# In whole tiles of the products by features, the high-part matmuls of both halves first, then the low-part ones of both

## The chip, the cores and the metric

The kernel runs on one NeuronCore of a Trainium2 chip. Its engines are TensorE (PE, with its weight loads PEld), VectorE (DVE), ScalarE (ACT), GpSimd (POOL) and SyncE (SP), which issues the transfers. Matmul results go to PSUM, which has eight banks of 128 partitions by 512 float32 columns. The metric is the device time in microseconds of one execution.

## The reference

A sequence of 256 positions with 1024 features, all float32, passes through two blocks. Of the first, two layers: attention over chunks of 64 frames, then a gated linear recurrence with a short convolution, each followed by an MLP with squared ReLU. The second block puts three mixers beside each other (gated linear attention, sparse attention that picks its keys by an index score, cross attention to 256 memory positions) and adds them by gates.

```
h  = h + attention(rmsnorm(h)) ; h = h + (relu(rmsnorm(h) @ w1) ** 2) @ w2
h  = h + rglru(rmsnorm(h))     ; h = h + (relu(rmsnorm(h) @ w1) ** 2) @ w2
u  = rmsnorm(x) @ w_in         # q, k, v, gates ... of three mixers, 11352 columns
x  = x + rmsnorm((s1 * y1 @ w1o + s2 * y2 @ w2o + s3 * y3 @ w3o) @ w_o)
```

Nearly all the work is products of a 256 x 1024 activation with weights. The result needs more precision than one fast matmul gives.

## The kernel before, in words

**Splitting.** Every operand is cut in a high part (rounded to the fast 32-bit format, `fp32r`) and a low part (the rest), and a product is the sum high x high + high x low + low x high. Weights come in tiles of 128 x 2048 (1 MB). SP loads a tile into one of five `raw` buffers. ACT makes `hi` of it (L822, two halves of a tile, three buffers `hi`), DVE makes `lo` (L1349, in place of `raw`). The semaphores `hi_cut` and `lo_cut` count these halves.

**Products by features.** Their output has features on the partitions and the 256 positions in the columns: q, k, w1 of the MLPs, rin, and most of the second block's first product. A tile holds the weights of 2 x 128 output features (j = 0, 1: the two halves in this case's words) for all 1024 input features, as NC = 8 blocks k of 128. The activation `X2` keeps for each block its high part and its low part side by side, 512 columns. So one matmul of 512 columns (`high`, L338) gives high x high in columns 0 to 255 of a bank and high x low in columns 256 to 511; one of 256 columns with the low weights (`low`, L346) adds low x high to columns 0 to 255. Each half of a tile takes 8 high and 8 low matmuls and has a bank of its own. `half` (L329) does one half: 7 highs, 8 lows, the last high. `cols` (L353) does a whole tile as two calls of `half`, one after the other.

**Draining.** When the last matmul of a bank tells `filled`, ACT copies columns 256 to 511 into a buffer `bt` (L853, three buffers), and DVE adds `bt` to columns 0 to 255 (`joined`, L1363 or, with a scale, L1365). DVE's sum tells `freed` of the bank. In `dv` it is ACT's copy alone that frees the bank (L833).

**Banks.** `fill(key, b)` makes PE wait until the bank's last contents have been drained (`freed[b]`), and books the next one. A `Side` object leaves out a wait that the same engine has passed before.

**Order.** Each engine has one queue, written out by hand in the program and worked in order. The ways in which `cols` follows other work on PE are:
- MLP: `cols` of w1 tile i, on banks (4,5) (tile 1 on (6,7)), then `rows` of w2 tile i-1 on banks 0 to 3 (24 matmuls of 512 columns, L293 to L295), then w1 tile i+1.
- rin 1 to 3: banks (2,3), (4,5), (2,3), with the small `gates` matmuls between.
- start of the second block: iq 0 on (4,5) (`cols_as_ready`), misc on bank 0, iq 1 on (4,5); index heads, dk and dq 0 half by half; dv on banks 4 and 5 (48 matmuls of 256 columns); then `cols` of dq 1, dq 2, gq 0, gq 1, gk 0, all on (4,5), and gk 1 on (0,1).
- dz 0 to 3: banks (4,5), (0,1), (4,5), (0,1), after the `gv` tiles.
- wk 0 on (4,5) and wq 0 on (7,6) near the start; xz 0 on (2,3), followed by xz 1's first half on bank 2.

In the stretch of dq, gq and gk DVE also takes maxima of the index scores (`top8`) after the two sums of each tile.

Of the kernel before, what the change touches and what calls it, by code (L numbers as in the profile page):

```python
# [8 lines left out]
P = 128  # L9
S = 256  # L10
D = 1024
NC = D // P
# [6 lines left out]
RAW, HIS, BT = 5, 3, 3  # L19
# [42 lines left out]
T_OF = {key: t for t, key in enumerate(PLAN)}  # L62
# [28 lines left out]
def build(nc, A, out):  # L91
    ctx = ExitStack()

    def sem(name):
        return ctx.enter_context(nc.semaphore(name))

    raw_in = [sem(f"raw_in{i}") for i in range(RAW)]
    hi_cut, lo_cut, tile_used = sem("hi_cut"), sem("lo_cut"), sem("tile_used")
# [44 lines left out]
    def place(name, off, free, dt=F32):  # L143
        return nc.alloc_sbuf_tensor_at(name, [P] + list(free), dt, offset=off)
# [5 lines left out]
    lo = [place(f"lo_{i}", o_raw + i * 8192, [TILE], F32R) for i in range(RAW)]  # L150
    hi = [place(f"hi_{i}", o_hi + i * 8192, [TILE], F32R) for i in range(HIS)]

    def slot(name, i, free=(NC, S), dt=F32, off=0):
        return place(name, o_slot[i] + off, free, dt)
# [63 lines left out]
    ik, low = slot("ik", 5, [S]), slot("low", 5, [S], off=1024)  # L218
# [30 lines left out]
    bank = [ctx.enter_context(nc.psum_tensor(f"bank{i}", [P, 512], F32)) for i in range(8)]  # L249
# [9 lines left out]
    full, free, bank_of, tile_end, bt_at = {}, {}, {}, {}, {}  # L259

    def cut_at(t, c):

        return 2 * (t - 2) + c + 1
# [7 lines left out]
    def pe():  # L271
        PE = nc.tensor
        p = Side(PE)
# [3 lines left out]
        def fill(key, b, read=None):  # L277
            if b in read_by:
                p.wait_ge(*read_by.pop(b))
            p.wait_ge(freed[b], reads[b])  # L280
            fills[b] += 1
            full[key], bank_of[key] = (filled[b], fills[b]), bank[b]
            if key[0] in ROWS_ADDED:
                read_by[b] = (h_added, ROWS_ADDED[key[0]] + b + 1)
            elif read:
                read_by[b] = read
            else:
                reads[b] += 1
                free[key] = (freed[b], reads[b])
            return filled[b]  # L290

        def mm3(o, ah, al, bh, bl, start, stop):
            PE.matmul(o, ah, bh, start=start, stop=False)  # L293
            PE.matmul(o, ah, bl, start=False, stop=False)  # L294
            return PE.matmul(o, al, bh, start=False, stop=stop)  # L295
# [33 lines left out]
        def half(name, i, j, x, b, ks=range(NC), last=False):  # L329
            t = T_OF[name, i]  # L330
            if ks[0] == 0:
                fill((name, 2 * i + j), b)
            wh, wl = hi[t % HIS], lo[t % RAW]

            def high(k_):
                p.wait_ge(hi_cut, cut_at(t, k_ // 4))
                c = k_ * 256 + j * 128
                return PE.matmul(bank[b][:, :], wh[:, c:c + P], x[:, k_, :, :].rearrange("p a b -> p (a b)"),  # L338
                                 start=k_ == 0, stop=k_ == NC - 1, skip_group_check=True)

            for k_ in ks[:-1]:
                high(k_)
            for k_ in ks:
                p.wait_ge(lo_cut, cut_at(t, k_ // 4))
                c = k_ * 256 + j * 128
                PE.matmul(bank[b][:, 0:S], wl[:, c:c + P], x[:, k_, 0, :], start=False, stop=False, skip_group_check=True)  # L346
            m = high(ks[-1])
            if ks[-1] == NC - 1:
                m.then_inc(filled[b], 1)
                if j == 1 or last:  # L350
                    tile_end[t] = full[name, 2 * i + j]

        def cols(name, i, x, banks):  # L353
            half(name, i, 0, x, banks[0])
            half(name, i, 1, x, banks[1])

        def cols_as_ready(name, i, x, banks, split):
            t = T_OF[name, i]
# [144 lines left out]
        total("mix0", 0)  # L503
        p.wait_ge(ident_in, 16)
        cols("wk", 0, X2, (4, 5))
        cols("wq", 0, X2, (7, 6))
        for b in range(4):
            p.wait_ge(*free["wv", b])
# [29 lines left out]
        for j in range(9):  # L538
            name, i = ATTN_TILES[j]
# [22 lines left out]
        def mlp(n, fill_i):  # L562
            p.wait_ge(x_low, low_at("mem", NC - 1))
            half("mk", fill_i, 0, M2, 7)
            turned_x(f"mlp{n}", h, h_added, 8 * n)
            half("mk", fill_i, 1, M2, 6)
            for i in range(17):
                if i == 0:
                    cols_as_ready(f"w1_{n}", 0, X2, (4, 5), f"mlp{n}")
                elif i < 16:  # L570
                    cols(f"w1_{n}", i, X2, (6, 7) if i == 1 else (4, 5))
                if i > 0:
                    p.wait_ge(z_low, 32 * n + 2 * i)
                    rows(f"w2_{n}", i - 1, 16, zh[(i - 1) % 3], zl[(i - 1) % 3])
# [40 lines left out]
        done = fill(("iw", 0), 1)  # L615
        for j in range(2):
            m = PE.transpose(bank[1][:, 32 * j:32 * j + 32], low[0:32, j * P:(j + 1) * P], ident[0:32, 0:32])
# [18 lines left out]
        t = T_OF["dv", 0]  # L636
        for j in range(2):
            done = fill(("dv", j), 4 + j)
            for k_ in range(NC):
                p.wait_ge(lo_cut, cut_at(t, k_ // 4))  # L640
                w, r = slice(k_ * 256, (k_ + 1) * 256), slice(j * P, (j + 1) * P)
                m = mm3(bank[4 + j][:, 0:S], xh[:, k_, r], xl[:, k_, r], hi[t % HIS][:, w], lo[t % RAW][:, w],
                        k_ == 0, k_ == NC - 1)
# [25 lines left out]
        for i in range(10):  # L669
# [11 lines left out]
            if i >= 2:  # L681
                n = i - 2
                c = (n // 4) * 128
                p.wait_ge(*free["turn", 16 + n])
                done = fill(("dav", n), 7)
# [48 lines left out]
        for i in range(6):  # L734
# [5 lines left out]
            if i < 4:  # L740
                p.wait_ge(mk_low, i + 1)
                p.wait_ge(xq_low, i + 1)
                done = fill(("s", 24 + i), 4)
                for j, c in ((1, 0), (0, 256)):
                    for k_ in range(2):
# [3 lines left out]
                        m = PE.matmul(o, xql[:, n, r], mkh[:, n, :], start=False, stop=k_ == 1, skip_group_check=True)  # L749
# [3 lines left out]
            if i >= 2:  # L753
# [3 lines left out]
                for m_ in range(2):  # L757
                    b = 6 + m_
                    done = fill(("xo", 2 * n + m_), b)
                    c = n * 256 + m_ * P  # L760
                    for j in range(2):
                        r = slice(j * 256, j * 256 + 256)
                        m = mm3(bank[b][:, 0:S], mvh[:, j, c:c + P], mvl[:, j, c:c + P], pth[n % 2][:, r], ptl[n % 2][:, r], j == 0, j == 1)
# [26 lines left out]
        for s_, c in ((0, 0), (0, 1), (1, 0), (1, 1)):  # L790
            r = slice(s_ * P, (s_ + 1) * P)
            for i in (2, 3):
                t = T_OF["wf", i]
                p.wait_ge(f_low, i + 1)
                for k_ in range(2):
                    p.wait_ge(lo_cut, cut_at(t, k_))
                    w = slice(k_ * D + c * 512, k_ * D + (c + 1) * 512)
                    m = mm3(bank[2 * c + s_][:, :], fh[:, 2 * i + k_, r], fl[:, 2 * i + k_, r], hi[t % HIS][:, w], lo[t % RAW][:, w],
                            False, i == 3 and k_ == 1)
# [1370 lines left out]
```

## Time and profile before

| | us |
|---|---|
| three runs | 977.11, 977.18, 975.89 (median 977.11) |
| profiled execution, its span | 975.9 |
| PE busy | 968.3 (99%) |
| PEld busy | 826.0 (85%) |
| DVE busy | 680.5 (70%) |
| ACT busy | 588.6 (60%) |
| matmuls L338, x1016, mean 394 ns | 266.3 |
| matmuls L346, x1016, mean 282 ns | 141.6 |

The times of the runs lie within 1.3 us. The profiled execution's time is its span, 975.9, and no more stands beside it: the lowest of the three runs, 975.89, agrees with it. The duration of a matmul is modelled and overlaps the next one, so the distance of two starts is what a matmul costs, not its 394 or 282 ns. The profile groups matmuls of one line that follow each other: "209.35 2.00 PE L338 ... x8" is the last high of one half and the first seven of the next.

### The profile page before, as it was taken

The page shows a single profiled execution, that of the slowest core. Times are in us where ns is not written, and L with a number is a line of the kernel's source. Part 1 is how long each engine was busy: PE and PEld are TensorE (multiplying, and loading weights), DVE is VectorE, ACT ScalarE, POOL GpSimd, SP SyncE. Part 2 cuts the span into 40 slices and gives each one's busy share as a digit, 9 for nine tenths or more (in the row PEclk, how much of TensorE's full clock was granted, in tenths as well). Part 3 has the DMA queues.
Part 4 walks back from the last instruction along what each step waited for, and adds up shares of the span by engine and source line. Part 5 has one row for each costly group of instructions (what it writes and reads, how often), then busy time and mean ns, then how long its engine had stood idle before and what let it go on. Part 6 is the DMA issues. An engine that isn't in the chain of part 4 may idle for free.

```text
span 975.9 us, 13399 instructions
## 1 busy us (share of the span) xinstructions
PE 968.3 (99%) x5146; PEld 826.0 (85%) x5146; DVE 680.5 (70%) x1161; ACT 588.6 (60%) x1042; POOL 66.2 (7%) x80
## 2 busy tenths in 40 slices
PE   8999999999999999999999999999999999999997
PEld 6887788888888898888888888888888888988886
DVE  5877786666568789666665588778767554877564
ACT  6777755454457897645454467547876555684443
POOL 1322110000000242000000000000011000000000
PEclk9999999999999999999999999999999999999999
DMA  9753545655455445555655556445543544335551
GB/s 368 296 194 134 184 173 186 224 176 211 174 196 185 146 165 192 182 187 184 226 178 207 177 198 250 173 175 188 198 165 105 193 148 170 132 133 209 177 189 44
DMA packets 27119, 180.33 MB, mean 185 GB/s; under 512 B 2992, under 2 KB 3888, under 8 KB 6320
## 3 DMA queue, kind: packets, MB, share of 16 engines
q1 hardware_dynamic: 26336, 176.98, 50.7%
q0 software_dynamic: 288, 2.10, 0.6%
q8 instruction: 41, 0.67, 0.3%
q10 hardware_dynamic: 432, 0.39, 0.1%
q14 instruction: 22, 0.18, 0.0%
HBM read 178.41 MB, written 1.05 MB: 184 GB/s over the span
## 4 chain that ended last, share of the span: by engine, by line
PE 99%; DMA 1%; DVE 0%; ACT 0%; SPq 0%; issue 0%; DVEq 0%
PE bank L338 25%; PE bank L293 16%; PE bank L295 16%; PE bank L294 16%; PE bank L346 13%; PE bank L308 1%; PE bank L468 1%; PE bank L484 1%; PE bank L589 1%; PE bank L518 1%; PE bank L309 1%; DMA front<-in_front 1%; PE bank L529 1%; PE bank L404 0%; PE bank L399 0%; PE bank L400 0%
## 5 line engine op out<-in xcount | busy, mean ns | idle before, releaser
L1349 DVE TENSOR_TENSOR lo<-raw,hi 128x1024 fp32r<-128x1024 f32 x318 | 375.9, 1229 | 20.1 <-ACT hi L822 19.9
L822 ACT ACTIVATE hi<-raw 128x1024 fp32r<-128x1024 f32 x318 | 320.3, 1050 | 100.1 <-PE bank L295 98.2
L338 PE MATMUL bank<-X,hi 128*128 128x512 f32 x1016 | 266.3, 394 | 0.0
L338 PEld LDWEIGHTS bank<-X,hi 128*128 128x128 f32 x1016 | 185.0, 189 | 32.8
L346 PEld LDWEIGHTS bank<-X,lo 128*128 128x128 f32 x1016 | 138.5, 190 | 10.1
L346 PE MATMUL bank<-X,lo 128*128 128x256 f32 x1016 | 141.6, 282 | 0.0
L853 ACT ACTIVATE bt<-bank 128x256 f32<-128x256 f32 x135 | 51.0, 380 | 141.5 <-PE bank L338 133.1
L1363 DVE TENSOR_TENSOR zr<-bank,bt 128x256 f32<-128x256 f32 x64 | 27.2, 424 | 108.9 <-ACT bt L853 108.9
L293 PE MATMUL bank<-hi,zh 128*128 128x512 f32 x256 | 100.0, 390 | 0.0
L295 PE MATMUL bank<-hi,zl 128*128 128x512 f32 x256 | 99.8, 390 | 0.0
L294 PE MATMUL bank<-lo,zh 128*128 128x512 f32 x256 | 99.6, 389 | 0.0
L293 PE MATMUL bank<-hi,X 128*128 128x512 f32 (+1 forms) x176 | 67.9, 386 | 0.0
L295 PE MATMUL bank<-hi,X 128*128 128x512 f32 (+1 forms) x176 | 66.9, 380 | 0.0
L294 PE MATMUL bank<-lo,X 128*128 128x512 f32 (+1 forms) x176 | 66.8, 380 | 0.0
L295 PEld LDWEIGHTS bank<-hi,zl 128*128 128x128 f32 x256 | 48.1, 188 | 10.4
L294 PEld LDWEIGHTS bank<-lo,zh 128*128 128x128 f32 x256 | 48.1, 188 | 10.2
L293 PEld LDWEIGHTS bank<-hi,zh 128*128 128x128 f32 x256 | 48.2, 188 | 8.8
L997 ACT ACTIVATE zh<-zf 128x256 fp32r<-128x256 f32 x64 | 26.6, 416 | 21.3 <-DVE zf L1520 21.3
L295 PEld LDWEIGHTS bank<-hi,X 128*128 128x128 f32 x176 | 33.1, 188 | 6.4
L293 PEld LDWEIGHTS bank<-hi,X 128*128 128x128 f32 x176 | 33.1, 188 | 6.2 <-issue 0.3
L294 PEld LDWEIGHTS bank<-lo,X 128*128 128x128 f32 x176 | 33.1, 188 | 6.0
L907 ACT ACTIVATE L<-L,stat 128x256 f32<-128x256 f32 (+1 forms) x56 | 25.5, 457 | 20.4 <-DVE stat L1482 9.8
(345 smaller groups left out, 1420.5 us busy)
## 6 DMA issues: line engine op xcount, KB each, us to landing
raw<-in_w SPq DMA_DIRECT2D x64, 1024.0 KB, 4.7
raw<-in_rin SPq DMA_DIRECT2D x8, 1024.0 KB, 4.8
raw<-in_wk SPq DMA_DIRECT2D x4, 1024.0 KB, 10.3
raw<-in_wq SPq DMA_DIRECT2D x4, 1024.0 KB, 8.3
raw<-in_wo SPq DMA_DIRECT2D x4, 1024.0 KB, 4.7
raw<-in_mk SPq DMA_DIRECT2D x4, 1024.0 KB, 4.8
raw<-in_mv SPq DMA_DIRECT2D x4, 1024.0 KB, 4.8
raw<-in_rout SPq DMA_DIRECT2D x4, 1024.0 KB, 4.6
```

The source lines that it names most:

```text
L293: PE.matmul(o, ah, bh, start=start, stop=False)
L294: PE.matmul(o, ah, bl, start=False, stop=False)
L295: return PE.matmul(o, al, bh, start=False, stop=stop)
L308: PE.matmul(bank[b][:, :], wh[:, c:c + P], both_, start=k_ == 0, stop=False, skip_group_check=True)
L338: return PE.matmul(bank[b][:, :], wh[:, c:c + P], x[:, k_, :, :].rearrange("p a b -> p (a b)"), start=k_ == 0, stop=k_ == NC - 1, skip_gro ...
L346: PE.matmul(bank[b][:, 0:S], wl[:, c:c + P], x[:, k_, 0, :], start=False, stop=False, skip_group_check=True)
L822: ACTE.activation(hi[u_ % HIS][:, c], raw[u_ % RAW][:, c], ACT.Copy).then_inc(hi_cut, 1)
L853: ACTE.activation(bt[n % BT][:, :], bank_of[key][:, S:2 * S], func, scale=scale, **kw).then_inc(bt_made, 1)
L907: i = ACTE.activation(Lb[:, c:e], Lb[:, c:e], ACT.Exp, scale=-1.0, bias=s_[:, m:m + 1], accum_out=s_[:, 2 + m:3 + m])
L997: ACTE.activation(zh[i % 3][:, j, :], zf[c % 4][:, :], ACT.Copy).then_inc(z_high, 1)
L1349: DVE.tensor_tensor(lo[u_ % RAW][:, c], raw[u_ % RAW][:, c], hi[u_ % HIS][:, c].bitcast(F32), ALU.subtract).then_inc(lo_cut, 1)
L1363: DVE.tensor_tensor(dst, first, rest, ALU.add).then_inc(free[key][0], 1)
```

## The change

`cols` no longer calls `half` twice. It fills both banks first, then issues 8 highs into the first bank, 7 into the second, 8 lows into the first (the last of them tells `filled` of the first bank), 8 lows into the second, and the second bank's last high, which tells `filled` of the second. The matmuls, their operands and their count are the same; within a bank the sums are added in another order. `half` stays as it is for the tiles that are done half by half. The lines of the kernel after the change stand 26 lower from here on, and the whole tiles' highs and lows are now on L362 and L368.

```diff
@@ -351,8 +351,34 @@
                     tile_end[t] = full[name, 2 * i + j]
 
         def cols(name, i, x, banks):
-            half(name, i, 0, x, banks[0])
-            half(name, i, 1, x, banks[1])
+
+            t = T_OF[name, i]
+            wh, wl = hi[t % HIS], lo[t % RAW]
+            done = [fill((name, 2 * i + j), banks[j]) for j in range(2)]
+
+            def high(j, k_):
+                p.wait_ge(hi_cut, cut_at(t, k_ // 4))
+                c = k_ * 256 + j * 128
+                return PE.matmul(bank[banks[j]][:, :], wh[:, c:c + P], x[:, k_, :, :].rearrange("p a b -> p (a b)"),
+                                 start=k_ == 0, stop=j == 1 and k_ == NC - 1, skip_group_check=True)
+
+            def low(j, k_):
+                p.wait_ge(lo_cut, cut_at(t, k_ // 4))
+                c = k_ * 256 + j * 128
+                return PE.matmul(bank[banks[j]][:, 0:S], wl[:, c:c + P], x[:, k_, 0, :], start=False,
+                                 stop=j == 0 and k_ == NC - 1, skip_group_check=True)
+
+            for k_ in range(NC):
+                high(0, k_)
+            for k_ in range(NC - 1):
+                high(1, k_)
+            for k_ in range(NC):
+                m = low(0, k_)
+            m.then_inc(done[0], 1)
+            for k_ in range(NC):
+                low(1, k_)
+            high(1, NC - 1).then_inc(done[1], 1)
+            tile_end[t] = full[name, 2 * i + 1]
 
         def cols_as_ready(name, i, x, banks, split):
             t = T_OF[name, i]
```

PE's order at the passage from dq 1 to dq 2, where both tiles use banks 4 and 5. Names: `hi_2_61` is the tile's high part in the third `hi` buffer, `lo_2_56` its low part, `X2_91` the activation; a bracket holds the semaphores that the row waits for. Before:

```order
L338 MATMUL bank5<-X2_91,hi_1_60 128x512
L338 MATMUL bank4<-X2_91,hi_2_61 128x512 [waits hi_cut,freed4]
L338 MATMUL bank4<-X2_91,hi_2_61 128x512 x3
L338 MATMUL bank4<-X2_91,hi_2_61 128x512 [waits hi_cut]
L338 MATMUL bank4<-X2_91,hi_2_61 128x512 x2
L346 MATMUL bank4<-X2_91,lo_2_56 128x256 [waits lo_cut]
L346 MATMUL bank4<-X2_91,lo_2_56 128x256 x3
L346 MATMUL bank4<-X2_91,lo_2_56 128x256 [waits lo_cut]
L346 MATMUL bank4<-X2_91,lo_2_56 128x256 x3
L338 MATMUL bank4<-X2_91,hi_2_61 128x512
L338 MATMUL bank5<-X2_91,hi_2_61 128x512 [waits freed5]
```

After the change, the same passage:

```order
L368 MATMUL bank5<-X2_91,lo_1_55 128x256 x8
L362 MATMUL bank5<-X2_91,hi_1_60 128x512
L362 MATMUL bank4<-X2_91,hi_2_61 128x512 [waits hi_cut,freed5,freed4]
L362 MATMUL bank4<-X2_91,hi_2_61 128x512 x3
L362 MATMUL bank4<-X2_91,hi_2_61 128x512 [waits hi_cut]
L362 MATMUL bank4<-X2_91,hi_2_61 128x512 x3
L362 MATMUL bank5<-X2_91,hi_2_61 128x512 x7
```

What moved: the wait for `freed5` stood before the second half's first high, 7 highs and 8 lows and one high into dq 2, and now stands with `freed4` at dq 2's first matmul. The second bank's highs follow the first's without lows between.

PE's order in the first MLP, from the middle of a w1 tile (banks 4, 5) to the w2 rows behind it (bank 0, with `zh`, `zl`: the two parts of the squared ReLU). Before:

```order
L346 MATMUL bank4<-X2_91,lo_0_54 128x256 [waits lo_cut]
L346 MATMUL bank4<-X2_91,lo_0_54 128x256 x3
L338 MATMUL bank4<-X2_91,hi_0_59 128x512
L338 MATMUL bank5<-X2_91,hi_0_59 128x512 [waits freed5]
L338 MATMUL bank5<-X2_91,hi_0_59 128x512 x6
L346 MATMUL bank5<-X2_91,lo_0_54 128x256 x8
L338 MATMUL bank5<-X2_91,hi_0_59 128x512
L293 MATMUL bank0<-hi_1_60,zh0_124 128x512 [waits lo_cut,z_low]
```

After the change:

```order
L362 MATMUL bank5<-X2_91,hi_0_59 128x512 x7
L368 MATMUL bank4<-X2_91,lo_0_54 128x256 [waits lo_cut]
L368 MATMUL bank4<-X2_91,lo_0_54 128x256 x3
L368 MATMUL bank4<-X2_91,lo_0_54 128x256 [waits lo_cut]
L368 MATMUL bank4<-X2_91,lo_0_54 128x256 x3
L368 MATMUL bank5<-X2_91,lo_0_54 128x256 x8
L362 MATMUL bank5<-X2_91,hi_0_59 128x512
L293 MATMUL bank0<-hi_1_60,zh0_124 128x512 [waits lo_cut,z_low]
```

What moved: two runs of highs and two of lows are now one of each, with one high at the end; the rows of w2 behind the tile, and what they wait for, stand as before.

## Rows read from the trace of the kernel before

**Rows 1.** The page, busy time by engine, and its chain by engine
```profile
PE 968.3 (99%) x5146; PEld 826.0 (85%) x5146; DVE 680.5 (70%) x1161; ACT 588.6 (60%) x1042; POOL 66.2 (7%) x80
...
PE 99%; DMA 1%; DVE 0%; ACT 0%; SPq 0%; issue 0%; DVEq 0%
```

**Rows 2.** Waits of PE and its weight loads: us in total, times, longest
```profile
PE bank L496 <- POOL warm L1995: 1.3, 1, 1.3
PE bank L378 <- ACT hi L920: 1.1, 1, 1.1
...
PEld bank L293 <- DVE lo L1349: 0.3, 1, 0.3
```

**Rows 3.** Order of time on PE, an MLP tile: start, us, engine, line, idle before
```profile
206.81 1.75 PE L338 MATMUL bank<-X,hi 128*128 128x512 f32 x7
208.39 1.12 PE L346 MATMUL bank<-X,lo 128*128 128x256 f32 x8
209.35 2.00 PE L338 MATMUL bank<-X,hi 128*128 128x512 f32 x8
211.19 1.11 PE L346 MATMUL bank<-X,lo 128*128 128x256 f32 x8
...
212.37 0.40 PE L293 MATMUL bank<-hi,zh 128*128 128x512 f32 x1
```

**Rows 4.** Busy time by stretches: PE, PEld, DVE, ACT, POOL, granted clock, DMA
```profile
0.00:10.00 10.00, 7.53 (x19) 4.23 (x20) 3.10 (x7) 4.65 (x8) 0.74 (x5) 1.00 0.80 291
...
629.00:658.00 29.00, 29.00 (x169) 25.55 (x168) 19.46 (x43) 13.65 (x21) 0.00 (x0) 1.00 0.51 181
```

**Rows 5.** Order of time on PE, from dv to gk 0
```profile
623.76 0.28 PE L293 MATMUL bank<-hi,X 128*128 128x256 f32 x1
...
629.52 1.78 PE L338 MATMUL bank<-X,hi 128*128 128x512 f32 x7
...
634.88 2.00 PE L338 MATMUL bank<-X,hi 128*128 128x512 f32 x8
...
640.47 2.00 PE L338 MATMUL bank<-X,hi 128*128 128x512 f32 x8
...
657.23 2.00 PE L338 MATMUL bank<-X,hi 128*128 128x512 f32 x8
```

**Rows 6.** Order of time on DVE, bank 5 drained after that MLP tile
```profile
201.96 0.42 DVE L1363 TENSOR_TENSOR zr<-bank,bt 128x256 f32<-128x256 f32 x1 [1.91 <-ACT bt L853]
```

**Rows 7.** DVE's sums of iq 0, and PE at the start of iq 1
```profile
602.23 0.76 DVE L1363 TENSOR_TENSOR iq<-bank,bt 128x256 f32<-128x256 f32 x2
...
603.09 2.00 PE L338 MATMUL bank<-X,hi 128*128 128x512 f32 x8
```

**Rows 8.** Order of time on ACT at dq 1 and dq 2
```profile
629.72 0.38 ACT L833 ACTIVATE dv<-bank 128x256 f32<-128x256 f32 x1 [2.49 <-PE bank L295]
...
635.32 0.38 ACT L853 ACTIVATE bt<-bank 128x256 f32<-128x256 f32 x1 [2.41 <-PE bank L338]
```

**Rows 9.** Order of time on DVE at dq 1 and dq 2
```profile
635.73 0.43 DVE L1365 SCALAR_TENSOR_TENSOR dq<-bank,bt 128x256 f32<-128x256 f32 x1 [2.37 <-ACT bt L853]
...
641.32 0.42 DVE L1365 SCALAR_TENSOR_TENSOR dq<-bank,bt 128x256 f32<-128x256 f32 x1 [1.39 <-ACT bt L853]
```

**Rows 10.** ACT's release and PE's restart near 9 us
```profile
8.57 0.61 ACT L920 ACTIVATE hi<-front 128x512 fp32r<-128x512 f32 x1
...
9.24 0.73 PE L378 MATMUL bank<-hi,X 128*128 128x512 f32 x2 [1.14 <-ACT hi L920]
9.81 0.40 PE L381 MATMUL bank<-hi,X 128*128 128x512 f32 x1
```

**Rows 11.** PE at xz 0 and xz 1, and DVE's second sum
```profile
822.66 1.75 PE L338 MATMUL bank<-X,hi 128*128 128x512 f32 x7
...
827.99 1.32 PE L338 MATMUL bank<-X,hi 128*128 128x512 f32 x5
...
828.84 0.42 DVE L1363 TENSOR_TENSOR zx<-bank,bt 128x256 f32<-128x256 f32 x1 [2.08 <-ACT bt L853]
```

## The prediction

> **What bounds the kernel now.** I read the page first: matmuls fill 968.3 of 975.9 us and the chain that ended last is 99% PE [rows 1]. Busy PE alone proves little, since matmuls are pipelined, so next I read what PE waited for: two waits in the whole execution, the longest 1.3 us, for the first constants and for the first `hi` [rows 2]. Then the order of time inside a tile: matmuls of 512 columns start 0.227 us apart (7 from 206.81 to 208.39) and those of 256 columns 0.12 us apart (8 from 208.39 to 209.35), with nothing between them [rows 3]. The granted clock is 1.00, the 2.4 GHz level [rows 4]. So PE's instruction stream is the bound. Work of ACT and DVE counts only where it makes PE wait, and a PE wait anywhere is added to the end, because no later slack can swallow it.
>
> **What is only moved.** Each of the 47 whole tiles keeps its 32 matmuls: 16 high ones of 512 columns, 16 low ones of 256. (wk 1, wq 1, w1 of both MLPs 30, rin 3, iq 1, dq 2, gq 2, gk 2, dz 4, xz 1.) No other engine gets or loses an instruction, and no DMA is touched. Three things change: how often PE passes from a low run into a high run, when the first bank is complete, and when the second bank has to be free.
>
> **Term 1, runs.** After a low run the highs come a little slower: 8 from 209.35 to 211.19 take 1.84 us, against 8 x 0.2266 = 1.81 at the pace of the 7 before [rows 3]. Seen by halves: first high 206.81, first high of the second half 209.35 + 0.23 = 209.58, next group of rows 212.37, so 2.77 us for the half that starts clean and 2.79 for the one that starts behind lows. The change takes one such passage out of each tile, the one in its middle; that at its end stays. 47 x 0.02 = 0.94, or 1.03 with the unrounded starts behind these rows. I take -1.0 us. Bounds: nothing (0) and, if both the passages of a tile went, -2.1. The longer low run of 16 should cost nothing of its own: 48 matmuls of 256 columns from 623.76 to 629.52 are 0.120 apart too [rows 5].
>
> **Term 2, low parts later.** The lows start after 15 highs in place of 7, 1.8 us later, so VectorE's `lo` gets more time. The only wait for `lo` is one of 0.3 us before a weight load of L293, the products by rows [rows 2], none in these tiles, so this gives 0.
>
> **Term 3, the second bank.** `half` asked for its bank when it began; `cols` now asks for both before its first matmul. The order of PE shows this: `freed5` moves from the middle of the tile to its first row. It is asked for 2.77 us sooner. Where another group of matmuls lies between two uses of the bank this is free. In the MLPs, DVE frees bank 5 at 201.96 + 0.42 = 202.38, and the next `w1` tile starts at 206.81 [rows 3, 6]: 4.4 us to spare, 30 tiles alike but for the alternation at i = 1. `dz` alternates (4,5) and (0,1), so that a whole tile of 5.6 us lies between two uses of a bank. iq 1: 602.23 + 0.76 = 602.99 against 603.09 + 0.23 = 603.32 [rows 7].
> It is not free where tiles on banks (4,5) stand back to back: dv, dq 1, dq 2, gq 0, gq 1, gk 0. That is five entries.
> - dv to dq 1: dq 1 starts at 629.52 [rows 5]; bank 5 holds dv's second half, which ACT copies from 629.72 for 0.38, free at 630.10 [rows 8]. PE would idle 0.58 us.
> - dq 1 to dq 2: the last high of dq 1 starts at 634.88, the first of dq 2 at 635.11 [rows 5]. The bank is freed by two engines in turn: ACT's `bt` at 635.32 for 0.38 [rows 8], DVE's sum at 635.73 for 0.43, free at 636.16 [rows 9]. PE would idle 1.05 us. Gq 0 repeats it: last high 640.47 [rows 5], DVE done 641.32 + 0.42 [rows 9]; gq 1 and gk 0 have the same distance. Four entries. DVE is free when `bt` comes: the first half's sum will start some 4.9 us into the tile and end 0.7 us before the second's is due.
>
> Restart: the second wait of [rows 2], in mid-work, shows it. ACT's `hi` ends at 8.57 + 0.61 = 9.18, matmul restarts at 9.24 and the next two starts lie 0.57 us on, not 0.45, since the first weight load was not under a matmul [rows 10]. So about 0.05 + 0.11 = 0.16 us each. The highs after an idle PE do not pay the 0.03 of term 1. Sum: (0.58 + 0.16 - 0.03) + 4 x (1.05 + 0.16 - 0.03) = 0.71 + 4.72 = +5.4 us. Bounds: without any restart +4.6; with twice that restart +6.2.
>
> The TensorE page of the Trainium skill ("TensorE: Matmul & The Clock Gate", Part 2, LDWEIGHTS step) says that PE's queue can pull weight loads ahead of matmuls in flight. If it did so past a wait for a bank, 0.11 of each restart would go and the sum would be 0.55 us less. [Rows 10] speak against it: there the next two starts come 0.57 us on, the time of one load over the usual.
>
> **Term 4, the first bank.** It is complete after 15 highs and 8 lows, 15 x 0.2266 + 8 x 0.12 = 4.35 us into the tile; before it was 2.77. Its drain ends about 1.2 us after its last matmul starts, so 5.4 us in, and the tile lasts 5.56. Only xz 0 is followed at once by a user of its first bank: start 822.66, last low 826.90, `bt` 827.22, DVE from 827.63 (idle there, 2.08 us before 828.84) to 828.05; xz 1 starts at 828.20 [rows 11]. That is just in time; if the weight load has to wait too it costs 0.05. I take 0, bound +0.3. Elsewhere ACT and DVE drain the pair closer together, but the last drain of a tile hangs on the second half, whose end stays: `z` in the MLP waits for it, k and q in the attention, the taps of rin.
>
> **Sum.** -1.0 + 0 + 5.4 + 0 = +4.4 us against the profiled execution's 975.9, its span, which agrees with the lowest of the three times (975.89); so 980.3. The median of the runs is 977.1, 1.2 above, so a median of 981.5. Bounds: -2.1 + 4.6 = +2.5 and 0 + 6.2 + 0.3 = +6.5.
>
> **Rivals.**
> - A, not slower: the early wait has no price. The place is the start of dq 1, dq 2, gq 0, gq 1 and gk 0; it decides if bank 5 is free within 0.23 us of the last high's start. Then term 1 alone is left, 977.1 - 1.0 = 976.1. For it: PE shows no bank wait now. Against it: ACT's `bt` starts 0.43 us after that high's start (634.88 to 635.32) and two operations of 0.4 us follow each other [rows 5, 8, 9]; it can't be free before 1.2. Chance 0.05. To gain more, all passages between runs would have to cost over 0.11 us a tile (5.4 / 47), and the rows have 0.05 at most; 0.02 for that, at 974.9.
> - B, clock: a PE that idles 1.2 us in each 6.7 loses granted clock in this stretch. Price: work of 28 us (five tiles, 629.52 to 657.23 + 0.23 [rows 5]) at the 1.2 GHz level takes twice as long, +28 us if all of it, +7 for a quarter; with term 3, 988 to 1010. Against it: PE idled 1.14 us before 9.24 and the granted clock is 1.00 in 0 to 10 us as well [rows 4, 10]. Chance 0.04. The same page of the Trainium skill, in its section on a second HAM failure mode, says that small idles between groups of matmuls can make the clock swing; by that rule this rival would hold.
> - C, more entries bite than the five: iq 1 (0.33 us to spare), xz 1 (0.15), or VectorE behind at one of them, since its queue is in order and it now drains both halves together. Up to 1.2 us each, +1 to +3 over the forecast, 982.5 to 984.5. Against it: DVE's rows show idle time before both sums there [rows 9]. Chance 0.12.
> - D, that the change does not do what it says: the order of PE shows it does; 0.
>
> **Numbers.** The forecast, 979.5 to 983.5 around 981.5, has 0.77; A 0.05 and 0.02, B 0.04, C 0.12. The range for 8 in 10 takes the bounds of the terms (+2.5 to +6.5: 979.6 to 983.6), half of C, and the 0.6 us by which medians may lie apart: 979.2 to 984.3. A change of 0.2%, 1.95 us, is what a measurement of this kernel can tell from none. Slower by more: the forecast but for its lowest edge, B and C, 0.91; within: A and that edge, 0.07; faster 0.02.
>
> **What would show it.** In the profile after: idle time of PE or its weight loads before the high matmuls of five tiles between 629 and 665 us, released by DVE `dq`, `gq` (ACT `dv` the first time), 0.6 once and about 1.1 four times; tile starts there 6.7 us apart, not 5.59. In the MLP a `w1` tile of 5.54 plus 0.02 us, and stage starts some 0.8 us earlier by 600 us. Wrong would be: no such waits (A), a granted clock under 1 (B), waits in `w1`, iq or xz tiles (C), or a low run of 16 slower than 1.92 us, which would undo term 1.

## The result, and the profile after

The changed kernel takes 982.11 us (median of five runs, 981.48 to 982.30), the kernel before 977.18 us in the same session. The ratio is 1.0049, interval [1.0037, 1.0061]: 0.5% slower. The profiled execution of the changed kernel spans 980.8 us at a granted clock of 1.00, that of before 975.9.

The page after: the busy time by engine, one group of matmuls, and the shares of the chain that ended last.

```profile
PE 969.7 (99%) x5146; PEld 826.8 (84%) x5146; DVE 680.9 (69%) x1161; ACT 589.4 (60%) x1042; POOL 66.3 (7%) x80
...
PE 98%; DMA 1%; issue 0%; DVE 0%; ACT 0%; SPq 0%; DVEq 0%
...
L362 PE MATMUL bank<-X,hi 128*128 128x512 f32 x752 | 186.6, 391 | 4.4 <-issue 4.4
```

The work is the same (5146 matmuls, as in [rows 1]). New is the idle time of 4.4 us before the highs of the whole tiles. The waits after, first PE's, then the first row of its weight loads (us in total, times, longest):

```profile
PE bank L362 <- issue: 4.4, 5, 1.0
PE bank L522 <- POOL warm L2021: 1.3, 1, 1.3
PE bank L404 <- ACT hi L946: 0.3, 1, 0.3
...
PEld bank L362 <- issue: 5.8, 5, 1.3
```

Against [rows 2] one wait is new, and it comes five times. The profile names no releaser ("issue" is time for which it shows no reason), so the list alone doesn't say what PE waited for. PE in order of time, from dq 1 to gk 0, does better:

```profile
628.90 0.28 PE L295 MATMUL bank<-hi,X 128*128 128x256 f32 x1
629.71 3.68 PE L362 MATMUL bank<-X,hi 128*128 128x512 f32 x15 [0.52 <-issue]
633.22 2.08 PE L368 MATMUL bank<-X,lo 128*128 128x256 f32 x16
635.14 0.39 PE L362 MATMUL bank<-X,hi 128*128 128x512 f32 x1
636.51 3.65 PE L362 MATMUL bank<-X,hi 128*128 128x512 f32 x15 [0.98 <-issue]
...
641.91 0.39 PE L362 MATMUL bank<-X,hi 128*128 128x512 f32 x1
643.28 3.67 PE L362 MATMUL bank<-X,hi 128*128 128x512 f32 x15 [0.98 <-issue]
646.78 2.08 PE L368 MATMUL bank<-X,lo 128*128 128x256 f32 x16
...
656.83 3.65 PE L362 MATMUL bank<-X,hi 128*128 128x512 f32 x15 [0.98 <-issue]
...
662.23 3.14 PE L362 MATMUL bank<-X,hi 128*128 128x512 f32 x13
```

The five idles stand at the first highs of dq 1, dq 2, gq 0, gq 1 and gk 0, one of 0.52 and four of 0.98. (The view counts an idle from the modelled end of the matmul before, 0.39 us after its start; the next high could have started 0.23 after it, so an idle of 0.98 keeps PE 1.14 longer.) Tile starts lie 6.8 us apart where they lay 5.59 apart [rows 5]. Who ends such an idle is seen at gq 0, by the same view of the weight loads, ACT and DVE:

```profile
643.25 0.76 PEld L362 LDWEIGHTS bank<-X,hi 128*128 128x128 f32 x4 [1.26 <-issue]
```
```profile
641.15 0.38 ACT L879 ACTIVATE bt<-bank 128x256 f32<-128x256 f32 x1 [3.31 <-PE bank L368]
642.34 0.38 ACT L879 ACTIVATE bt<-bank 128x256 f32<-128x256 f32 x1 [0.81 <-PE bank L362]
```
```profile
641.57 0.42 DVE L1391 SCALAR_TENSOR_TENSOR dq<-bank,bt 128x256 f32<-128x256 f32 x1 [1.72 <-ACT bt L879]
642.75 0.42 DVE L1391 SCALAR_TENSOR_TENSOR dq<-bank,bt 128x256 f32<-128x256 f32 x1 [0.76 <-ACT bt L879]
```

The last high of dq 2 starts at 641.91. ACT copies from 642.34, DVE adds from 642.75 and is done with bank 5 at 643.17. The weight load starts at 643.25 and the matmul at 643.28: unrounded, 0.07 and 0.10 behind the sum's end. These answer to [rows 8, 9], with the same distances (high to `bt` 0.43, `bt` to sum 0.41): the drain hasn't changed, only the moment at which PE asks for the bank.

The MLP tile, PE in order of time, against [rows 3]:

```profile
206.82 3.56 PE L362 MATMUL bank<-X,hi 128*128 128x512 f32 x15
210.22 2.08 PE L368 MATMUL bank<-X,lo 128*128 128x256 f32 x16
212.13 0.40 PE L362 MATMUL bank<-X,hi 128*128 128x512 f32 x1
212.36 0.40 PE L293 MATMUL bank<-hi,zh 128*128 128x512 f32 x1
```

The tile takes 212.36 - 206.82 = 5.54 us, before 212.37 - 206.81 = 5.56. From one w1 tile's start to the next (tile and w2 rows, 26 such steps in the two MLPs, each within 0.001 of the mean) it is 11.007 us after and 11.027 before: 0.020 won. Its start stands where it stood, because this execution was 0.2 us behind in the first ten us (9.42 for the matmul that started at 9.24 in [rows 10]) and has won that back over the tiles since.

**Where the 4.9 us went.** Matched matmul by matmul, the changed kernel is 0.19 us late at 10 us, 0.50 early at dv, 5.00 late at gk 1, 4.9 at xz 0 and 4.95 at the end. So the five entries cost 5.5 us net, the 36 whole tiles ahead of them win 0.71, 0.0196 each, and what is left is the start: from the 10th us to the end the change costs 4.77. Busy time by engine in this stretch shows nothing but idle PE (30.57 us busy of 35); the granted clock, the third number from the end, is 1.00:

```profile
629.00:664.00 35.00, 30.57 (x169) 25.94 (x168) 20.23 (x47) 14.64 (x22) 0.00 (x0) 1.00 0.45 152
```

### The profile page after: what moved, and what is told of

It is laid out like the page before. It is cut to its first block, busy times and chain, and to the rows that moved or that the text cites. A ratio compares the mean times of both kernels' runs of the same rounds, so it can differ in the third digit from the quotient of the medians.

```text
span 980.8 us, 13401 instructions
## 1 busy us (share of the span) xinstructions
PE 969.7 (99%) x5146; PEld 826.8 (84%) x5146; DVE 680.9 (69%) x1161; ACT 589.4 (60%) x1042; POOL 66.3 (7%) x80
## 3 DMA queue, kind: packets, MB, share of 16 engines
HBM read 178.41 MB, written 1.05 MB: 183 GB/s over the span
## 4 chain that ended last, share of the span: by engine, by line
PE 98%; DMA 1%; issue 0%; DVE 0%; ACT 0%; SPq 0%; DVEq 0%
PE bank L362 18%; PE bank L293 16%; PE bank L295 16%; PE bank L294 16%; PE bank L368 9%; PE bank L338 8%; PE bank L346 4%; PE bank L308 1%; PE bank L494 1%; PE bank L510 1%; PE bank L615 1%; PE bank L544 1%; DMA front<-in_front 1%; PE bank L309 1%; PE bank L555 1%
## 5 line engine op out<-in xcount | busy, mean ns | idle before, releaser
L362 PE MATMUL bank<-X,hi 128*128 128x512 f32 x752 | 186.6, 391 | 4.4 <-issue 4.4
L362 PEld LDWEIGHTS bank<-X,hi 128*128 128x128 f32 x752 | 140.7, 188 | 32.9 <-issue 5.8
L368 PEld LDWEIGHTS bank<-X,lo 128*128 128x128 f32 x752 | 96.4, 191 | 3.7
L368 PE MATMUL bank<-X,lo 128*128 128x256 f32 x752 | 97.5, 283 | 0.0
L338 PE MATMUL bank<-X,hi 128*128 128x512 f32 x264 | 72.5, 401 | 0.0
L338 PEld LDWEIGHTS bank<-X,hi 128*128 128x128 f32 x264 | 47.5, 189 | 8.2
```

The lines of the kernel that those rows point to most:

```text
L362: return PE.matmul(bank[banks[j]][:, :], wh[:, c:c + P], x[:, k_, :, :].rearrange("p a b -> p (a b)"), start=k_ == 0, stop=j == 1 and k_ = ...
L368: return PE.matmul(bank[banks[j]][:, 0:S], wl[:, c:c + P], x[:, k_, 0, :], start=False, stop=j == 0 and k_ == NC - 1, skip_group_check=True)
```

## The experiments

All nine edits concern `cols` or the banks it is given; none leaves work out. The first four ran on one chip beside the kernel before (977.24), the next four on one beside it again (977.37), the ninth beside 977.23. In the changed kernels' lists of waits below, those for the first constants and the first `hi` are left out.

**e1: the new order, the second bank asked for when its first high comes.**

```diff
-            done = [fill((name, 2 * i + j), banks[j]) for j in range(2)]
+            done = [fill((name, 2 * i), banks[0])]
...
             for k_ in range(NC):
                 high(0, k_)
+            done.append(fill((name, 2 * i + 1), banks[1]))
```

> The new order of highs and lows, but PE asks for the second bank only before that bank's first high, 8 highs (1.8 us) into the tile. Bank theory (the loss is the early question for the second bank): the five waits between 629 and 660 us are gone, since a bank is free about 1.28 us after its last high starts and is now asked for 2.0 us after it; what is left is the gain of one passage from lows to highs in each of 47 tiles, 47 x 0.02 = 0.94 us, less 0.05 at xz 1: 0.9 us under the kernel before, 976.3. Order theory (the loss comes from the long runs and from ACT and DVE draining both halves together): PE still idles in this stretch and the time stays near 982.

Measured: 975.87 us, ratio 0.9988 [0.9979, 0.9997], span 975.0, no wait for a bank in the list. PE at the same place:

```profile
628.58 0.28 PE L295 MATMUL bank<-hi,X 128*128 128x256 f32 x1
628.70 3.59 PE L362 MATMUL bank<-X,hi 128*128 128x512 f32 x15
632.13 2.08 PE L368 MATMUL bank<-X,lo 128*128 128x256 f32 x16
634.04 3.85 PE L362 MATMUL bank<-X,hi 128*128 128x512 f32 x16
637.73 2.08 PE L368 MATMUL bank<-X,lo 128*128 128x256 f32 x16
```

Asking eight matmuls later takes the whole loss away and leaves a gain: 1.4 us in the medians, with 0.9 us of uncertainty, and 0.67 us between the 10th us and the end of the profiled executions, matmul by matmul. The order of the matmuls isn't what costs.

**e2: the old order, both banks asked for at the start.**

```diff
-            half(name, i, 0, x, banks[0])
-            half(name, i, 1, x, banks[1])
+            for j in range(2):
+                fill((name, 2 * i + j), banks[j])
+            half(name, i, 0, x, banks[0], filled_before=True)
+            half(name, i, 1, x, banks[1], filled_before=True)
```

> The order of the kernel before (7 highs, 8 lows, a high, twice), but both banks are asked for ahead of the tile's first matmul. Bank theory: the same five waits as in the changed kernel, 0.6 and four of 1.1 us with restart, +5.5 us in all and none of the gain of the runs: 982.7, some 0.9 above the changed kernel. The first bank is drained early here, so xz 1 doesn't wait. Order theory: no loss to speak of, 977 to 978.

Measured: 982.82 us, ratio 1.0058 [1.0045, 1.0071], span 981.5. Its waits:

```profile
PE bank L338 <- issue: 4.4, 5, 1.0
...
PEld bank L338 <- issue: 5.8, 5, 1.3
```

The same five waits, the same 4.4 and 5.8 us, without any reordering: the early asking alone makes them. The two experiments and the two kernels make a square: asked for late, old and new order take 977.2 and 975.9; asked for early, 982.8 and 982.1. The early asking costs 5.6 in the old order and 6.2 in the new; the new order gains 1.4 and 0.7, which at this uncertainty are one number. Matched matmul by matmul from the 10th us on, the square closes better: the early asking costs 5.54 in the old order and 4.77 + 0.67 = 5.44 in the new, the new order gains 0.67 and 5.54 - 4.77 = 0.77.

**e3: the changed kernel, with dq 1, gq 0 and gk 0 on banks 2 and 3.**

```diff
-            cols("dq", i, X2, (4, 5))
+            cols("dq", i, X2, (2, 3) if i == 1 else (4, 5))
...
-            cols("gq", i, X2, (4, 5))
+            cols("gq", i, X2, (4, 5) if i else (2, 3))
...
-        cols("gk", 0, X2, (4, 5))
+        cols("gk", 0, X2, (2, 3))
```

> The changed kernel with both banks asked for at the tile's start, but dq 1, gq 0 and gk 0 on banks (2,3), dq 2 and gq 1 on (4,5), so that no bank is used twice in a row. Bank theory: PE asks for banks that were last used a tile (5.5 us) ago and finds them free; no waits, 0.9 us under the kernel before, 976.3, the same as with the late question. If the question itself cost time at each of the 47 tiles, or if draining both halves together did, this one would stay above the kernel before.

Measured: 976.01 us, ratio 0.9989 [0.9980, 0.9998]. PE in this stretch:

```profile
632.90 3.82 PE L362 MATMUL bank<-X,hi 128*128 128x512 f32 x16
636.56 2.08 PE L368 MATMUL bank<-X,lo 128*128 128x256 f32 x16
638.47 3.82 PE L362 MATMUL bank<-X,hi 128*128 128x512 f32 x16
```

Still asked for early, but the bank was last used a tile ago: no wait, tile starts 5.57 apart. It is the bank's return that decides, not the wait as an instruction. (The span of this execution, 973.7, flatters it by 1.3 us that it won in the first ten us; its median doesn't show them. From there on it gains 0.85.)

**e4: asked for after 4 highs.**

```diff
             for k_ in range(NC):
+                if k_ == 4:
+                    done.append(fill((name, 2 * i + 1), banks[1]))
                 high(0, k_)
```

> The new order, with the second bank asked for after 4 highs (0.91 us into the tile). Bank theory: a bank is free 1.28 us after its last high starts; PE comes to the question 0.23 + 0.91 = 1.14 us after it, so four waits shrink to 0.14 plus the restart (0.10 until the matmul starts and 0.08 for the weight load), about 0.3 each, 1.2 in all, and the one behind dv (free 0.58 us into the tile) is gone: 977.2 - 0.9 + 1.2 = 977.5. If instead a wait has a fixed price whatever its length, the loss would stay near 5 us or vanish whole.

Measured: 977.68 us, ratio 1.0005 [0.9996, 1.0014]. The list of PE's waits shows nothing here; that of its weight loads does, and the order of time says how long:

```profile
PEld bank L362 <- DVE dq L1393: 0.9, 2, 0.4
PEld bank L362 <- DVE gq L1391: 0.9, 2, 0.4
```
```profile
634.30 4.14 PE L362 MATMUL bank<-X,hi 128*128 128x512 f32 x16
638.27 2.08 PE L368 MATMUL bank<-X,lo 128*128 128x256 f32 x16
```

Sixteen highs take 3.97 us where e1's take 3.69: 0.28 for each of four entries, 1.1 in all, and the matched matmuls are 1.13 later over the stretch. (dq 1, where the bank is back sooner, has none.) Three points give the curve of one entry, each set against e1's tile starts of 5.60: asked for after no highs 1.19 us (tile starts 6.78 apart in the changed kernel), after four 0.28, after eight nothing. Between the first two it falls by 0.91, for 4 x 0.227 = 0.91 us of later asking: one for one.

**e5: the old halves in shorter runs, 4 highs, 4 lows, 3 highs, 4 lows, 1 high.** This asks what the 0.02 of term 1 hangs on.

```diff
-            for k_ in ks[:-1]:
-                high(k_)
-            for k_ in ks:
...
+            n = len(ks) // parts
+            for at in range(0, len(ks), n):
+                for k_ in ks[at:at + n]:
+                    if k_ != ks[-1]:
+                        high(k_)
+                for k_ in ks[at:at + n]:
...
-            half(name, i, 0, x, banks[0])
-            half(name, i, 1, x, banks[1])
+            half(name, i, 0, x, banks[0], parts=2)
+            half(name, i, 1, x, banks[1], parts=2)
```

> The kernel before, but each half of a whole tile as 4 highs, 4 lows, 3 highs, 4 lows, a high: four passages from lows to highs in a tile in place of two, banks asked for as before. If each passage costs 0.02 us, whatever the length of the low run, the time rises by 2 x 0.02 x 47 = 1.9 us to 979.1. If the price grows with the low run before it, half the run has half the price and the time stays at 977.2. If the order of highs and lows has no price at all, 977.2 too, and the highs behind lows show no slower starts.

Measured: 977.19 us beside 977.37, ratio 1.0000 [0.9992, 1.0009]. The MLP tile:

```profile
206.65 1.07 PE L338 MATMUL bank<-X,hi 128*128 128x512 f32 x4
207.56 0.64 PE L349 MATMUL bank<-X,lo 128*128 128x256 f32 x4
208.03 0.86 PE L338 MATMUL bank<-X,hi 128*128 128x512 f32 x3
208.73 0.64 PE L349 MATMUL bank<-X,lo 128*128 128x256 f32 x4
209.20 1.32 PE L338 MATMUL bank<-X,hi 128*128 128x512 f32 x5
...
212.24 0.40 PE L293 MATMUL bank<-hi,zh 128*128 128x512 f32 x1
```

The step from one w1 tile to the next is 11.033 us, 0.007 over before, with four low runs in a tile in place of two. Two passages more for 0.007: a fixed 0.020 for each is out. Taken at 0.020 behind eight lows (term 1), the mean of these four is (0.040 + 0.007) / 4 = 0.012. But the edit shortens two things, the runs of lows and the runs of highs behind them, and this mean doesn't tell which counts. The distances of single starts say more (unrounded, mean of 27 w1 tiles). In the kernel before, the highs behind eight lows start 233, 236, 228, 233 and 231 ns apart before they are back at 227: 28 ns lost. The lows behind highs start 113 and 119 ns apart before they are at 120: 8 won, which leaves the 0.020. In e5 the three highs behind the first four lows start 233, 236 and 228 ns apart, as slow as behind eight, and then the next lows end the run. At the tile's end, where w2's long run of 512 columns follows in both kernels, two starts are late behind four lows (236, 233, then 227) and five behind eight. So less is lost for both reasons: the highs are cut off, and fewer of them are late.

**e6: one high, one low, in turn** (the same edit with `parts=8`).

> The kernel before, but each half as high, low, high, low in turn (only its last two lows stand together). Fixed price a passage (0.02 us): 12 more a tile, 12 x 0.02 x 47 = 11 us, 988.5. Price by the length of the low run: a high behind one low starts some 0.006 us late, as in the tiles that take one high and one low in turn already (0.352 us a pair against 0.347), 14 x 0.006 x 47 = 3.9 us, less the two passages of the kernel before, 1.9: 979.2. A wait for low parts that are asked for 7 highs (1.6 us) sooner would show beside it; none is expected.

Measured: 979.47 us, ratio 1.0025 [1.0016, 1.0034].

```profile
206.99 0.39 PE L338 MATMUL bank<-X,hi 128*128 128x512 f32 x1
207.22 0.28 PE L349 MATMUL bank<-X,lo 128*128 128x256 f32 x1
207.33 0.40 PE L338 MATMUL bank<-X,hi 128*128 128x512 f32 x1
...
212.62 0.40 PE L293 MATMUL bank<-hi,zh 128*128 128x512 f32 x1
```

The tile has 14 low runs, and the step from tile to tile is 11.080 us, 0.053 over before: (0.040 + 0.053) / 14 = 0.007 for a passage behind one low, or two. A fixed 0.02 for each would have made a kernel of 988.5. So the price of a passage is not fixed. The means 0.007, 0.012 and 0.020 belong to these three patterns; they are not shown to be a law of the low run's length, since only one high follows each low here. At the tile's end, behind two lows and with a long run of 512 columns following, the starts are 236, 233, then 227, as behind four. In the changed order the highs behind sixteen lows start 233, 236, 228, 233 and 231 ns apart, just as behind eight: beyond eight the length of the low run adds nothing. That is why one run of 16 in place of two of 8 gains 0.020.

**e7: e1 with xz 0 done by halves.** This one is for term 4.

```diff
-        cols("xz", 0, X2, (2, 3))
+        half("xz", 0, 0, X2, 2)
+        half("xz", 0, 1, X2, 3)
```

> The late question of the first experiment, and xz 0 done half by half as in the kernel before, so that its first bank is complete after 2.8 us. The start of xz 1 loses its 0.05 us of lateness; 0.05 less than with the late question alone, less 0.02 for the passage that comes back: too little for the time, to be seen only in the distance of the starts there.

Measured: 976.79 us, one run. The seven highs at the start of xz 1, in e1 and then in e7 (there the first of the eight is xz 0's last high):

```profile
827.31 1.87 PE L338 MATMUL bank<-X,hi 128*128 128x512 f32 x7
829.02 1.10 PE L346 MATMUL bank<-X,lo 128*128 128x256 f32 x8
```
```profile
827.60 2.00 PE L338 MATMUL bank<-X,hi 128*128 128x512 f32 x8
829.44 1.11 PE L346 MATMUL bank<-X,lo 128*128 128x256 f32 x8
```

They take 1.71 in e1 and 1.84 - 0.23 = 1.61 in e7. Bank 2 is a shade late for xz 1 when xz 0 is done in the new order; with the 0.02 that the order gains at xz 0, that leaves a loss of some 0.06 to 0.08, too little for the time.

**e8: the new order in 42 tiles, the old one in the five back-to-back ones** (`cols_old` is `cols` as it was).

```diff
-            cols("dq", i, X2, (4, 5))
+            cols_old("dq", i, X2, (4, 5))
```

(and so for gq 0, gq 1 and gk 0)

> The changed kernel, but dq 1, dq 2, gq 0, gq 1 and gk 0 are done as in the kernel before; 42 tiles keep the new order and the early question for both banks. Bank theory: no wait anywhere but 0.05 at xz 1, and 42 x 0.02 = 0.84 us of gain: 976.4. If the early question costs anything in the 42 other tiles, it would show here as a time at or above 977.2.

Measured: 976.17 us, ratio 0.9991 [0.9982, 1.0000], no wait for a bank. All of the loss lies in five of the 47 tiles, and the others gain: 0.75 us from the 10th us on, matched matmul by matmul.

**e9: e7 with the banks of e3.** In e1 tile starts from dq 2 on lie 5.60 apart (634.04 to 639.64), no better than the old order's 5.59, while e3 has 5.57. Two reasons offered themselves.

> The changed order with the second bank asked for after 8 highs, dq 1, gq 0 and gk 0 moved to banks 2 and 3, and xz 0 done by halves, so that no tile asks for either of its banks within a few microseconds of their last use. Theory (the first bank, now complete only some 1.2 us before the tile's end, is late by a few hundredths at each of the back-to-back tiles, and that is why the late-asking kernel gained nothing there): the 16 highs behind a low run at dq 2 take 3.66 us, not 3.69, tile starts there lie 5.57 us apart, not 5.60, and from 617 to 657 us this kernel gains 0.10 us on the kernel before where the late-asking one lost 0.03. In time 0.85 to 1.1 us below the kernel before, 976.4 or less, and not to be told from the late-asking kernel. Rival (the missing gain came from asking for the second bank in mid-run, which splits the run of highs): tile starts stay 5.60 apart, because the second bank is still asked for in mid-run.

Measured: 976.12 us beside 977.23, ratio 0.9990 [0.9981, 0.9999].

```profile
634.47 3.82 PE L362 MATMUL bank<-X,hi 128*128 128x512 f32 x16
638.13 2.08 PE L368 MATMUL bank<-X,lo 128*128 128x256 f32 x16
640.04 3.82 PE L362 MATMUL bank<-X,hi 128*128 128x512 f32 x16
```

3.66 and 5.57, with the second bank still asked for in mid-run: the rival falls. From 617 to 657 us e9 gains the 0.10 that was expected, where e1 lost 0.03. In e1 it is the first bank that is late by a few hundredths at these entries, since in the new order it is complete 15 highs and 8 lows into its tile, 1.2 us before the tile's end. DVE frees it just behind that end (e1, DVE in order of time):

```profile
633.70 0.42 DVE L1392 SCALAR_TENSOR_TENSOR dq<-bank,bt 128x256 f32<-128x256 f32 x1 [3.30 <-ACT bt L880]
```

That is 634.12, while the last high has started at 634.04 and the next tile's first weight load is due under it. That load starts at 634.18 in e1, 0.14 behind the last high's start; in e9 it starts with the last high.

e1, e3, e8 and e9 all beat both kernels, by 0.1% over the one before, and their times can't be told apart. Matched matmul by matmul from the 10th us on (one execution each) they gain 0.67, 0.85, 0.75 and 0.93: e9, which leaves no bank late, gains the most. e1 is the least edit.

## Why the prediction was right

The time (981.5 forecast, 982.1 measured), its sign and its mechanism held. The sum was +4.4 us; from the 10th us on it is +4.77, made of 5.6 for the five entries, 0.05 at xz 1 and -0.9 for the order. The rest of the difference is the 0.19 of the first ten us and the spread of the medians. By its steps:

- **What bounds the kernel.** PE's stream, nothing else: every wait added is at the end in full. The matched matmuls are 5.00 us late at gk 1 and 4.95 at the end; nothing of it was given back. Shown.
- **Term 1, -1.0.** Matched matmuls gain 0.71 us over the 36 tiles ahead of dv, 0.0196 each, against 0.02 forecast. The size was right. A fixed price for each passage is not: e5 and e6 show means of 0.012 and 0.007 with shorter runs. The 0.02 held because the change does away with the very passages, behind eight lows, that it was read from.
- **Term 2, 0.** No wait for `lo` came into these tiles, and the low run of 16 took 212.13 - 210.22 = 1.91. Shown.
- **Term 3, +5.4.** Measured 5.5 net of 0.1 for the tiles' own gain, 5.6 gross. By parts, at one of the four: idle until the bank is free 643.18 - 642.14 = 1.04 (forecast 1.05); from there to the matmul 0.10 (0.05); the weight load that no matmul covers. Fifteen highs behind the restart take 646.78 - 643.28 = 3.50, in e1 behind dv 3.43, so 0.07 (0.11). Four times 1.04 + 0.10 + 0.07 = 1.21, and for dq 1 0.59 + 0.10 + 0.07 = 0.76, make 5.6. The forecast had 1.18 and 0.71. In part this is luck: of the restart the one half was too small by 0.05 and the other too large by 0.04. What failed a little is the sentence "the highs after an idle PE do not pay the 0.03": e1's 3.43 is 0.03 over the MLP tile's 3.40 (210.22 - 206.82), and 3.50 holds most of it too. Its starts lie 306 ns apart once, then 231, 236, 228, 233 and 230 before 227, as behind lows; at dq 2 only two of them are late (305, 233, 231, then 226). e1, e2, e3, e4 and e8 each show that the cause is the early asking for a bank that is still being drained.
- **The weight load pulled ahead.** The Trainium skill ("TensorE: Matmul & The Clock Gate", Step-by-step: what each phase is for) has PE pull weight loads ahead of matmuls in flight. Here the load at 643.25 came 0.07 behind the bank's release, as in all five entries, so it didn't pass this wait, and the 0.55 was not to be taken off. Between matmuls that wait for nothing the trace agrees: the load at 643.589 lies under the matmul that starts at 643.586, and its own matmul starts at 643.817.
- **Term 4, 0.** The value was near (0.05 at xz 1 in the matched matmuls, as the bound allowed), but the statement "only xz 0 is followed at once by a user of its first bank" was wrong: dq 1, dq 2, gq 0 and gq 1 are too, on bank 4. In the changed kernel the longer wait for bank 5 hides it; in e1 it shows (tile starts 5.60 apart, in e9 5.57), and eats the gain of the order there. (The rows put the start of xz 1 at 827.99 + 0.23 = 828.22, not 828.20, so the bank had 0.17 to spare.)
- **Rivals.** A fell by the five waits. B fell: 1.00 in 629 to 664 us with an idle of 0.98 us in each 6.8. The same page's section "A second HAM failure mode: psum-queue depth-cycling" says that small idles between groups of matmuls can make the clock swing; here they didn't. C fell but for those 0.05: none at iq 1, and DVE was idle 0.76 before the sum that frees bank 5. D fell by the rows after, which show 15 highs, 16 lows and a high, and the early wait.

## What to carry to other kernels

Where matmuls bound the kernel, ask for each result bank as late as its first write; a wait gathered at the head of a block is only free if the bank's last drain has ended by then. For each two tiles that share a bank, write down the time from its last matmul's start to its release (1.26 us here: 0.43 to ACT's copy, 0.41 from there to DVE's sum, 0.42 for the sum) and set it against the matmuls that stand between; reordering within a tile shifts both ends of this sum, for the first bank as well as the second. A change of order that gains by 0.02 us a tile can be outweighed by five places out of 47, so look at the exceptional neighbours, not the common ones.

## What the runs showed of the hardware that was not expected

- Behind eight or sixteen matmuls of 256 columns those of 512 columns start late five times (233, 236, 228, 233, 231 ns apart, then 227), and the first lows behind highs start a little early; the pair costs 0.020 us. With shorter runs it costs less on the mean, 0.012 in e5 and 0.007 in e6. The kernel shows the amount and not the reason, and no run varies the length of the lows alone.
- "issue" in a list of waits can be a semaphore's wait: all five idles stand there, and only the order of time on DVE names the releaser. Waits of 0.3 us or so (e4) are in no row of PE's list, only in that of its weight loads.
- Profiled executions differ by up to 1.6 us in the first 10 us (e3 was 1.27 early there, e7 0.38 late). The first `hi` kept PE waiting 1.1 us in the kernel before, 0.3 in the changed one, not at all in e3. A difference of spans under 1.6 us means nothing until that is taken off.
